# S5 mixer pieces three projection chunks later in a hand-written order, gated-unit halves one chunk apart

## The reference, cut to what matters

```
h = (_rms(x, p['norm_mix']) * (1.0 + sc1) + sh1).astype(dt)
z = h @ p['w_in']
xa, ga, gb, gc, xb, uc, q, k, v = jnp.split(z, 9, axis=-1)
...
bur = jnp.einsum('blgc,gpc->blgp', ug, bbr)       # S5: 16 groups of 16 channels, 64 complex states
_, _, hr, hi = lax.associative_scan(_cplx_combine, (are, aim, bur, bui), axis=1)
y = (einsum(hr, c_re) - einsum(hi, c_im)) + s5_d * uf
g = jax.nn.gelu(y) @ p['s5_glu_w'] + p['s5_glu_b']
out = g[..., :W] * jax.nn.sigmoid(g[..., W:])
```

## Time and profile before

| | |
|---|---|
| median of 3 runs | 2416.71 us (2412.31 to 2418.26) |
| the profiled execution: its time, its span | 2403.83 us, 2402.2 us |
| mean granted clock of PE | 0.946 of full speed |
| busy: PE, VectorE, ScalarE, POOL | 90%, 35%, 23%, 12% of the span |
| chain that ended last, by engine | PE 77%, VectorE 9%, DMA 5%, issue 4% |
| DMA | 438.91 MB, 183 GB/s over the span |

### The profile page before, as it was taken

How to read it: one execution, slowest core, us unless ns; L and a number is a source line. 1 busy time by engine, 2 the same in 40 slices (tenths; PEclk the granted TensorE clock), 3 DMA queues, 4 the chain that set the end, 5 groups by cost and what they waited for, 6 DMA issues and landing times.

```text
span 2402.2 us, 27992 instructions
## 1 busy us (share of the span) xinstructions
PE 2166.7 (90%) x7615; PEld 1092.0 (45%) x7616; DVE 852.5 (35%) x1969; ACT 562.8 (23%) x1110; POOL 284.8 (12%) x463
## 2 busy tenths in 40 slices
PE   3996999999989899999599299999999999999995
PEld 1343555544545665656244144444444444444342
DVE  3566554014572455565365511111111111111112
ACT  3410010225532434443122111111111111111111
POOL 0001020100010000001222211111111111111111
PEclk8998999999999589999899599999999999999998
DMA  9253131431546522223754635774479788687873
GB/s 376 93 215 60 54 70 54 169 98 70 136 161 192 180 65 104 100 91 139 246 209 156 216 128 162 274 251 150 155 262 335 268 325 321 215 309 270 308 251 70
DMA packets 122756, 438.91 MB, mean 183 GB/s; under 512 B 31955, under 2 KB 70579, under 8 KB 102115
## 3 DMA queue, kind: packets, MB, share of 16 engines
q1 hardware_dynamic: 92520, 309.99, 35.2%
q0 software_dynamic: 26032, 112.64, 17.4%
q10 hardware_dynamic: 4112, 15.14, 1.6%
HBM read 356.39 MB, written 83.10 MB: 183 GB/s over the span
## 4 chain that ended last, share of the span: by engine, by line
PE 77%; DVE 9%; DMA 5%; issue 4%; ACT 2%; POOL 1%; SPq 1%; DVEq 0%; ACTq 0%; POOLq 0%
PE bank L2550 20%; PE bank L2191 12%; PE bank L2578 10%; PE bank L2455 7%; PE bank L2554 4%; PE bank L2299 3%; PE bank L2354 3%; PE bank L2331 2%; PE bank L2581 2%; PE bank L2516 2%; PE bank L2341 2%; PE bank L2303 1%; PE bank L2271 1%; DMA arena<-xT 1%; DMA arena<-kc 1%
## 5 line engine op out<-in xcount | busy, mean ns | idle before, releaser
L2550 PE MATMUL bank<-arena 128*128 128x512 f32 x1120 | 491.0, 595 | 14.7 <-issue 14.7
L2191 PE MATMUL bank<-arena 128*128 128x512 f32 (+1 forms) x960 | 359.0, 533 | 9.6 <-ACTq L1066 9.6
L2550 PEld LDWEIGHTS bank<-arena 128*128 128x128 f32 x1120 | 211.9, 190 | 289.8 <-issue 289.8
L2578 PE MATMUL bank<-arena 128*128 128x512 f32 x560 | 249.6, 598 | 11.4 <-issue 11.2
L2191 PEld LDWEIGHTS bank<-arena 128*128 128x128 f32 x960 | 168.4, 191 | 193.9 <-issue 193.0
L2455 PE MATMUL bank<-arena 128*128 128x512 f32 x512 | 243.1, 599 | 0.0
L2083 DVE COPY arena<-bank 128x512 f32<-128x512 f32 x50 | 34.6, 693 | 550.3 <-PE bank L2565 550.3
L2578 PEld LDWEIGHTS bank<-arena 128*128 128x128 f32 x560 | 103.0, 189 | 135.1 <-issue 125.9
L2093 DVE TENSOR_TENSOR arena<-bank,arena 128x512 f32<-128x512 f32 (+1 forms) x50 | 34.5, 691 | 255.6 <-PE bank L2578 210.7
L2455 PEld LDWEIGHTS bank<-arena 128*128 128x128 f32 x512 | 87.8, 191 | 75.9 <-issue 75.8
L985 POOL DMA_INDIRECT o_y<-arena x50 | 79.3, 1586 | 307.5 <-issue 171.0
(11 more groups left out here) (475 smaller groups left out, 2562.2 us busy)
## 6 DMA issues: line engine op xcount, KB each, us to landing
arena<-wg SPq DMA_DIRECT2D x32, 2048.0 KB, 9.4
arena<-wu SPq DMA_DIRECT2D x32, 2048.0 KB
arena<-wd SPq DMA_DIRECT2D x32, 2048.0 KB, 8.1
arena<-mod_w SPq DMA_DIRECT2D x12, 2048.0 KB, 17.8
z_d<-arena ACTq DMA_DIRECT2D x12, 1056.0 KB, 6.4
arena<-z_d POOLq DMA_DIRECT2D x10, 1056.0 KB, 7.7
arena<-kc POOLq DMA_DIRECT2D x8, 1280.0 KB, 10.0
arena<-vc POOLq DMA_DIRECT2D x8, 1280.0 KB, 8.4
```

The source lines that it names most:

```text
L2191: ins = mm(bank[n % 2][:, 0:w], wz[:, i % 3, k, :], hT[:, k, t0:t0 + w], start=(k == 0), stop=(k == KT - 1))
L2550: ins = mm(bank[bk][:, :], xgT[:, s, k, :], m[w][:, k, :], start=(k == 0), stop=(k == KT - 1))
L2578: ins = mm(bank[4 + h][:, :], hhT[:, k, :], wd[w][:, k, 512 * h:512 * h + 512], start=(k == 0), stop=(k == 3))
```

## The change

Only the list is changed. For half 0 `s5prep` stands three chunks later, after (4, 2), and `s5a` 0, 0 after (5, 0) where it stood after (4, 1); the distances from there to `s5c` 0 are the same chunks in number and size. For half 1 `s5prep` stands after (7, 3) where it stood after (7, 0), and the pieces up to `s5c` 1 move alike, to after (10, 1) from after (9, 2); here some distances gain or lose a short chunk. `gluy` moves from after (10, 2) to after (11, 1), behind `wq`. `glu` 0 moves from after (10, 4) to after (11, 2), `tabl` from before it and ahead of `wq` to before it and behind `wq`. `glu` 1 stays after (11, 4). Between the two halves of the gated unit stand (11, 3) and (11, 4), one full chunk and the short one, where all of tile 11 stood. The order of the mixer's steps among each other is the same.

```
--- before.py
+++ after.py
@@ -330,11 +330,11 @@
 
         SCHEDULE = [("mod",), ("norm1",), *(("z", i, c) for c in range(3) for i in range(2)), ("modp", 0),
                     *(("z", i, c) for c in range(3, 5) for i in range(2)), ("s5par",), *zc(2), ("modp", 1), ("s5tab", 0), *zc(3),
-                    ("s5prep", 0), *zc(4, 0, 1), ("s5a", 0, 0), *zc(4, 2), ("s5a", 0, 1), *zc(4, 3), ("s5a", 0, 2),
-                    *zc(4, 4), *zc(5, 0), ("s5a", 0, 3), *zc(5, 1, 2), ("s5b", 0), *zc(5, 3, 4), *zc(6, 0), ("s5c", 0), ("s5tab", 1),
-                    *zc(6, 1, 2, 3, 4), *zc(7, 0), ("s5prep", 1), *zc(7, 1, 2, 3), ("s5a", 1, 0), *zc(7, 4), *zc(8, 0), ("s5a", 1, 1),
-                    *zc(8, 1), ("s5a", 1, 2), *zc(8, 2), ("s5a", 1, 3), *zc(8, 3, 4), ("s5b", 1), *zc(9, 0, 1, 2), ("s5c", 1),
-                    *zc(9, 3, 4), *zc(10, 0, 1, 2), ("gluy",), *zc(10, 3, 4), ("tabl",), ("glu", 0), *zc(11, 0, 1), ("wq",), *zc(11, 2, 3, 4), ("glu", 1),
+                    *zc(4, 0, 1, 2), ("s5prep", 0), *zc(4, 3, 4), *zc(5, 0), ("s5a", 0, 0), *zc(5, 1), ("s5a", 0, 1), *zc(5, 2), ("s5a", 0, 2),
+                    *zc(5, 3, 4), ("s5a", 0, 3), *zc(6, 0, 1), ("s5b", 0), *zc(6, 2, 3, 4), ("s5c", 0), ("s5tab", 1),
+                    *zc(7, 0, 1, 2, 3), ("s5prep", 1), *zc(7, 4), *zc(8, 0, 1, 2), ("s5a", 1, 0), *zc(8, 3, 4), ("s5a", 1, 1),
+                    *zc(9, 0), ("s5a", 1, 2), *zc(9, 1), ("s5a", 1, 3), *zc(9, 2), ("s5b", 1), *zc(9, 3, 4), *zc(10, 0, 1), ("s5c", 1),
+                    *zc(10, 2, 3, 4), *zc(11, 0, 1), ("wq",), ("gluy",), *zc(11, 2), ("tabl",), ("glu", 0), *zc(11, 3, 4), ("glu", 1),
                     ("gluo",), ("sqC",), *tile(0), *tile(1), ("tab",), ("outC",), ("Ac", 0), *tile(2), ("outCn",), ("A", 0), ("Aw", 0), ("Ac", 1),
                     *tile(3), ("tabs", 0), ("Ap", 0), ("As", 0), *tile(4), *tile(5), ("A", 1), ("Aw", 1), *tile(6), ("tabs", 1), ("Ap", 1), ("As", 1), *tile(7),
                     ("sqA",), ("B", 0), *tile(8), ("outA",), ("outAn",), *tile(9), ("tabs", 2), ("B", 1), *tile(10), ("sqB",), *tile(11), ("outB",),
```

## The result

| | before | changed |
|---|---|---|
| median, compared on the same chip | 2418.26 us (5 runs, 2412.31 to 2420.88) | 2394.19 us (5 runs, 2392.84 to 2399.99) |
| ratio of the times, 95% interval | | 0.9918 (0.9902 to 0.9933) |
| the profiled execution: time, span, clock | 2403.83, 2402.2 us, 0.946 | 2399.02, 2397.3 us, 0.944 |

The forecast was 2402 us with 2391 to 2412 around it; the change is faster, by 16 to 24 us as the interval has it. The two profiled executions differ by 4.8 us alone. That is no measure of the change: the profiled execution before was a short one, which the last experiments come back to. What the change does to the projection stage is read inside the stage. The head of the trace differs by up to 2 us between executions, so I measure from the end of the last chunk of tile 3 to the first matmul behind `glu` 1 (L2299).

A forecast was written before the change was run, and what follows sets the result against it. PE, busy 90% of the span, bounds the kernel, so only its idle and low-clock time can go: 24.3 - 7.0 (idle) - 2.4 (clock) - 0.3 (gelu) = 14.6 us, from median 2416.7 to 2402 us, range 2391 to 2412.

The forecast's parts named there:

- What could be removed: Projection stage, around the mixer's first half: PE's three idle times, 19.7 us, plus 4.6 us of low-clock excess, together 24.3 us.
- Both waits before `s5prep` 0 go: First half: PE's waits for VectorE, 12.66 us before the kernel matmuls and 4.37 us before the transposes, vanish.
- Rival 4: First half: `s5prep` 0 is late anyway because VectorE's preparation hangs on something moved; gain 0, 2417 us; chance 0.05.
- The `u` chain: First half, kernel matmuls through copies and `toep` DMAs to `u` loads: 1.1 us later, `s5a` possible at 239.4 us without other delay.
- The pair's delay: Tile 4's 1056 KB store and tile 7's 512 KB weight load delay first-half `u` loads by 4.0 us (0 to 4.9).
- Rival 1: First half: `u` loads don't suffer from the store; idle 3.0 us, no clock loss, gain 21.0 us, 2396 us; chance 0.18.
- the estimate of 13.6 us: The whole kernel's gain if, by the skill's packet turns, the `u` loads paid the full 4.9 us.
- The clock behind it: First-half `s5a`: after 7.0 us of idle time PE restarts at the low clock, costing 2.4 us.
- Second half: Mixer's second half: no new idle time; store and load fall on `toep` DMAs, 3.8 us cover, cost 0 (bound 1.1).
- The gated unit: From `s5c` 1 to `glu` 0: PE's 36.1 us against the gelu chain's 36.3; 0.3 us shows (0 to 1.5).
- rival 2: Gated unit: `wq` falls on the y loads, stall about 5 us plus 2.4 clock; gain 7.3 us, 2409 us; chance 0.14.
- Rival 3: Attention stage: low clock prolonged; 30 us more takes the whole gain, 45 us more gives 2424 us; chance 0.08.

The follow-up runs named there:

- the last experiments: The changed kernel and the kernel before, each run again unaltered: changed at ratio 0.9911 to before; before, one run, with a projection stage of 329.5 us.
- the kernel without brackets: Changed kernel with first-half steps from `s5a` 0,0 to `s5c` 0 one full chunk later and `s5prep` 1 after (7,4): ratio to before 0.9884, again 0.9901.
- the second execution: The changed kernel run once more, unaltered, against the kernel before: ratio 0.9911 (0.9891 to 0.9931), projection stage 314.5 us.
- the third: Changed kernel with tile 7's weight load meant for chunk (5,2), but issued when it was before, so in effect unaltered: ratio to before 0.9916.

## Why the prediction was right

**What could be removed** (24.3 us: 19.7 of idle time, 4.6 of low clock). Right: the kernel without brackets shows 24.5 us.

**Both waits before `s5prep` 0 go.** Right. Nothing stands before L2214 and L2223, and VectorE worked through as before (11.08 of 12 us for 10.97). Rival 4 is out.

**The `u` chain.** Copies 1.1 us later: the `u` issue is 228.96 - 219.19 = 9.77 us after `s5prep` 0; I had 226.73 + 1.1 - 218.10 = 9.73. PE comes to `s5a` 237.65 - 219.19 = 18.46 us after it, where I had 18.3. The pair's delay was mis-sized: 4.0 us taken, 2.7 measured. So the idle time is 5.59 us and not 7.0. Rival 1 (no delay, 3.0 us of idle time) is out too: postponing the pair brings 2.5 us back.
The Trainium skill (DMA: Bandwidth & Descriptors, section "Queues, rings and completion order") lets the queues take turns by packets. I had read from it that the whole 4.9 us of the pair would be paid; the stretches above show 2.7, so the estimate of 13.6 us (its own terms give 13.7) was too low, while the turns themselves are not contradicted.

**The clock behind it.** 2.4 us taken, 1.7 measured in the first execution, 3.0 in the second, 1.6 in the third. The term has a spread that I did not give it; with the idle time it is 7.3, 8.8 and 7.2 us against the 9.4 of the sum.

**Second half.** Right in its parts, and at the bound in one: the pair fell on the `toep` DMAs, POOL waited 6.64 us for them and 1.88 in the first half, 4.8 us more, nearly the whole 4.9. `u` was there 25.85 us after `s5prep` 1 and PE after 25.33, so 0.52 us shows where I took 0 with a bound of 1.1.

**The gated unit.** I took 0.3 us; 0 shows. The gelus end 35.4 us after `s5c` 1 and PE comes after 36.1: a cover of 0.7 us. What ends the gelus there is not the y chain of the prediction, though: it is ScalarE's place in the list, as the gelus start behind the copy of chunk (11,1) and the table load. In five of the seven traces of this order they end at the same 35.4 us, whether VectorE started with y after 24.9 us or after 26.4. VectorE's start came after 463.49 - 437.53 = 25.96 us, before it was 27.36 (457.60 - 430.24). With the gated unit alone, where the table load no longer stands at the chain's start and the stores are as before, it was 26.7, so the table load is 0.7 of the 1.4 us as far as single traces can say. `wq` went out at 463.71, after the y loads had landed, so rival 2 had no case here. In the second execution it went out at 464.22, 0.9 us before they had landed; the gelus ended 0.3 us later than in the first, and still in time.

**The sum.** 24.3 - 5.6 - 1.7 - 0.5 = 16.5 us by terms; 16.2 measured in the stage, 14.6 in the second execution and 16.5 in the third; I had 14.6. That the second execution meets it to the tenth is luck: its delay by the pair was smaller than the term, and its restart and its second half (0.6 us) were dearer. Rival 3 did not come in the size that it needed (30 us more of low clock), and the lead is kept. It is not empty, though. Worked out from the clock in stretches of 10 us from 740 to 900 us, the attention's start stood low for some 85 and 82 us in the two executions of before and for 92, 89 and 65 in the three of the changed kernel, and the attention took 334.8 and 335.0 us against 339.2, 339.2 and 330.2. With such a spread in one kernel a cost of some 4 us by the change is neither shown nor excluded.

**What stays open.** 16.2 us are 0.67% of the time, a ratio of 0.9933; 0.9918 was measured, 4 us more, and in the second comparison 0.9911, 7 us more than that execution's 14.6. The other comparisons with the later mixer come out at 0.9938 (0.9932 by their stage), 0.9916 (0.9932), 0.9923 (0.9935), 0.9884 and 0.9901 (0.9899): over all seven about 0.1% beyond the stage's gain, within most of the intervals. No profile shows a second place: behind the stage these seven traces take 1876 to 1889 us, 1883.5 in the mean, and the four with the order of before or one part of the change 1876 to 1886, 1882.6 in the mean. So the forecast's mechanism accounts for some 16 of the measured 16 to 24 us. The measured median lies near the low end of my range, and that end stood for all 24.3 us gone, which the changed kernel did not reach: that the time came out so low is not to the prediction's credit.

## What to carry to other kernels

When steps of a chain with latency (compute, DMA, DMA, compute) stand in a hand-written order between dense work, a gap is removed by moving the whole chain, and the chain's last member must move by the same time; moved in part, the wait reappears at the next half, or at the chain's end with a higher price. Before a move, list what large transfers the new neighbours issue, and leave the loads on the chain one chunk more than their lone latency: here the loads would have been 2.9 us late without their new neighbours, as they were 2.7 and 3.0 before at no loss of clock; with 2.7 us of DMA delay on top it was 5.6 us of idle time and a restart at the low clock, and one chunk more took both away. A postponed transfer is postponed only if what its engine waits for moves too: look for its new time in the trace before reading anything from such a kernel. Compare such an edit inside its stage, from one fixed point to another, since two whole executions of this kernel differ by 10 us where nothing was changed.

## What the runs showed of the hardware

- 1568 KB of large transfers (a 1056 KB store and a 512 KB load) cost 2.7 us beside the `u` loads of small packets, and 4.9 alone; the 512 KB load without the store cost them 1.7 (one execution). On the landing of the eight small `toep` DMAs the same pair cost 4.8 us.
- After a stop of PE of 4.8 to 5.9 us the clock was at its lower level in every profile, and the loss until it was back varied from 1.6 to 3.1 us, between executions of the same program too.
- The attention stage held the lower level for longer or shorter with nothing changed near it: 339.2, 339.2 and 330.2 us for the same work in three executions of the changed kernel. That is not all of the spread between executions: the two of before differ by 9.6 us, of which the attention has 0.2.
